# Pairing the 64-wide attention heads on TensorE and splitting the last norm by row blocks

## The reference

```python
h = x                                                   # (1, 256, 1024)
# layer 0
h = h + mixer_mla_retention(rmsnorm(h), ...)            # 8 MLA heads (96 q/k, 64 v), 8 retention heads (64 q/k, 128 v)
h = h + (silu(hn @ w_gate) * (hn @ w_up)) @ w_down      # D_FF = 3584
# layer 1
h = h + mixer_swa_stickbreak(rmsnorm(h), ...)           # 16 window heads and 8 stick-breaking heads, all 64 wide
h = h + moe(rmsnorm(h), ...)                            # top 2 of 8 experts, each SwiGLU with D_FF = 3584
return rmsnorm(h)

# one stick-breaking head, for each block of 128 queries
z = q @ k.T * scale
log_keep = where(before, log_sigmoid(-z), 0)
log_after = cumsum(log_keep, reverse) - log_keep
a = where(before, exp(log_sigmoid(z) + log_after), 0)
out = a @ v
```

## Time and profile before

| | us |
|---|---|
| median of 3 runs | 1602.17 (1601.64 to 1602.81) |
| the profiled execution, device time | 1601.8 |
| its span, first to last instruction | 1599.9 |
| TensorE busy | 1547.9 (97%) |
| TensorE weight loads busy | 1288.1 (81%) |
| VectorE busy | 1235.8 (77%) |
| ScalarE busy | 1085.4 (68%) |
| mean granted TensorE clock | 0.987 of full |

### The profile page before, as it was taken

How to read it: one execution, slowest core, us unless ns; L and a number is a source line. 1 busy time by engine, 2 the same in 40 slices (tenths; PEclk the granted TensorE clock), 3 DMA queues, 4 the chain that set the end, 5 groups by cost and what they waited for, 6 DMA issues and landing times.

```text
span 1599.9 us, 22666 instructions
## 1 busy us (share of the span) xinstructions
PE 1547.9 (97%) x7738; PEld 1288.1 (81%) x7738; DVE 1235.8 (77%) x1456; ACT 1085.4 (68%) x1309; POOL 25.9 (2%) x21
## 2 busy tenths in 40 slices
PE   7999899999999898999999999999999999999995
PEld 6777799999877677888888888888888888888884
DVE  3567544454556547999999999999999999999995
ACT  5555444444455436878878888888878778788874
POOL 0000000000000000000000000000000000000000
PEclk9999999999999998999999999999999999999998
DMA  8533465556443357999999999999999999999950
GB/s 318 184 106 108 138 229 184 184 184 211 159 157 106 118 181 279 365 383 349 399 383 351 393 386 351 395 385 350 394 387 350 392 388 350 394 387 353 404 208 28
DMA packets 193161, 454.90 MB, mean 284 GB/s; under 512 B 8144, under 2 KB 12112, under 8 KB 192848
## 3 DMA queue, kind: packets, MB, share of 16 engines
q1 hardware_dynamic: 190272, 443.69, 75.6%
q0 software_dynamic: 2832, 10.49, 2.6%
HBM read 447.33 MB, written 6.82 MB: 284 GB/s over the span
## 4 chain that ended last, share of the span: by engine, by line
PE 95%; DVE 3%; ACT 1%; issue 1%; DMA 0%; DVEq 0%; ACTq 0%; SPq 0%
PE bank L278 29%; PE bank L280 28%; PE bank L279 28%; PE bank L1757 2%; PE bank L356 1%; DVE w_lo L291 0%; PE bank L1205 0%; PE bank L763 0%; PE bank L752 0%; PE bank L337 0%; PE bank L1197 0%; PE bank L1198 0%; PE bank L357 0%; PE bank L1543 0%; PE bank L1536 0%
## 5 line engine op out<-in xcount | busy, mean ns | idle before, releaser
L291 DVE TENSOR_TENSOR w_lo<-ring,w_hi 128x1024 fp32r<-128x1024 f32 (+1 forms) x834 | 1006.8, 1220 | 255.4 <-ACT w_hi L287 208.9
L287 ACT ACTIVATE w_hi<-ring 128x1024 fp32r<-128x1024 f32 (+1 forms) x834 | 880.7, 1060 | 332.5 <-PE bank L280 332.2
L278 PE MATMUL bank<-w_hi,xe_hi 128*128 128x512 f32 x896 | 354.5, 396 | 3.2 <-DVE w_lo L291 1.8
L280 PE MATMUL bank<-w_hi,xe_lo 128*128 128x512 f32 x896 | 350.3, 391 | 0.0
L279 PE MATMUL bank<-w_lo,xe_hi 128*128 128x512 f32 x896 | 349.5, 390 | 0.0
L278 PEld LDWEIGHTS bank<-w_hi,xe_hi 128*128 128x128 f32 x896 | 168.7, 188 | 37.3 <-DVE w_lo L291 1.9
L280 PEld LDWEIGHTS bank<-w_hi,xe_lo 128*128 128x128 f32 x896 | 168.5, 188 | 36.2
L279 PEld LDWEIGHTS bank<-w_lo,xe_hi 128*128 128x128 f32 x896 | 168.9, 188 | 34.1
L278 PE MATMUL bank<-w_hi,hT_hi 128*128 128x512 f32 x448 | 177.5, 396 | 0.0
L280 PE MATMUL bank<-w_hi,hT_lo 128*128 128x512 f32 x448 | 176.0, 393 | 0.0
L279 PE MATMUL bank<-w_lo,hT_hi 128*128 128x512 f32 x448 | 175.7, 392 | 0.0
(11 more groups left out here) (297 smaller groups left out, 1474.9 us busy)
## 6 DMA issues: line engine op xcount, KB each, us to landing
ring<-m_gate_dram SPq DMA_DIRECT2D x112, 1024.0 KB, 6.0
ring<-m_up_dram SPq DMA_DIRECT2D x112, 1024.0 KB, 6.5
ring<-m_down_dram SPq DMA_DIRECT2D x112, 1024.0 KB, 6.4
ring<-f_gate_dram SPq DMA_DIRECT2D x14, 1024.0 KB, 5.0
ring<-f_up_dram SPq DMA_DIRECT2D x14, 1024.0 KB, 5.0
ring<-f_down_dram SPq DMA_DIRECT2D x14, 1024.0 KB, 4.9
ring<-ab_w_in_dram SPq DMA_DIRECT2D x12, 1024.0 KB, 5.6
ring<-cd_w_in_dram SPq DMA_DIRECT2D x11, 1024.0 KB, 5.0
```

The costliest lines, as they stand in the source:

```text
L278: nc.tensor.matmul(out_, a_hi, b_hi, start=first, stop=False, **kw)
L280: return nc.tensor.matmul(out_, a_lo, b_hi, start=False, stop=last, **kw)
L287: nc.scalar.activation(w_hi[:, buf, 0:width], src, ACT.Copy).then_inc(hi_ready, 1)
L291: nc.vector.tensor_tensor(w_lo[:, buf, 0:width], src, f32(w_hi[:, buf, 0:width]), ALU.subtract).then_inc(split_ready, 1)
```

## The change

1. `heads_out` becomes `pair_out`: it issues the value matmuls of two heads in turn, the first of the even head, the first of the odd head, then the second of each, into the two halves of one bank. MLA's, the window heads' and the stick-breaking heads' value pieces are called once for two heads.
2. The window heads' `scores` and the stick-breaking heads' `z_scores` are issued for two heads in turn, with one signal behind both. A second scores bank is added; the turned probabilities go to bank 6 (the last head's to bank 5) and the window heads' values to bank 7.
3. The pieces move to fit: window scores at odd steps for heads `d` - 7 and `d` - 6, values at even steps for `d` - 10 and `d` - 9; `z_scores` at steps 20, 22, 24, 26; `ln_part`, `softplus` and `log_after` for two heads at steps 21, 23, 25, 27; `masked` and `weights` at the even steps behind; `weigh` at 23, 25, 27, 29. In `ln_part` the three functions go through both heads in turn.
4. The count is waited for and loaded ahead of the last expert (`fullest`). The last norm waits block by block for `h`, squares into its own tile, takes two roots of one column, has its function table loaded ahead, and the result leaves in two DMAs.

The core of the diff:

```diff
+        def pair_out(bank, v, a):
+            for first in (True, False):
+                cols, src = (slice(0, 256), slice(0, 256)) if first else (slice(P, 256), slice(256, 384))
+                for r in range(2):
+                    ins = nc.tensor.matmul(pb[bank][half_rows(r), cols], v[r][0 if first else 1], a[r][:, src],
+                                           start=first, stop=not first, skip_group_check=True)
+            return ins
...
             def ln_part(j):
...
+                for i in (j, j + 1):
+                    act.wait_ge(z_banked, j + 2)
+                    if i >= 3:
+                        act.wait_ge(acc_banked, i - 2)
+                    as_(nc.scalar.activation(sb_sp[i % 3], pb[Z_BANKS[i % 2]][:, 0:384], ACT.Abs))
                 as_.settle()
-                as_(nc.scalar.activation(b, b, ACT.Exp, scale=-1.0))
+                for i in (j, j + 1):
+                    as_(nc.scalar.activation(sb_sp[i % 3], sb_sp[i % 3], ACT.Exp, scale=-1.0))
                 as_.settle()
-                nc.scalar.activation(b, b, ACT.Ln, bias=1.0).then_inc(ln_done, 1)
+                for i in (j, j + 1):
+                    nc.scalar.activation(sb_sp[i % 3], sb_sp[i % 3], ACT.Ln, bias=1.0).then_inc(ln_done, 1)
...
             def weigh(j):
-                pe.wait_ge(a_done, j + 1)
-                if j % 2 == 0 and j:
+                pe.wait_ge(a_done, j + 2)
+                if j:
                     pe.wait_ge(mixT_done, KM + 8 + j // 2)
+                else:
+                    pe.wait_ge(pT_done, MLA_H + SWA_H - 1)
...
+            for tb in range(TB):
+                act.wait_ge(sc_done, 4 + 2 * tb + 2)
+                nc.scalar.activation(squares, h[:, tb, :], ACT.Square, accum_out=ss[:, tb:tb + 1]).then_inc(sq_done, 1)
+                act.wait_ge(sq_done, 8 + tb + 1)
+                nc.scalar.activation(rms[:, tb:tb + 1], ss[:, tb:tb + 1], ACT.Sqrt, bias=const("eps", 0, 1),
+                                     scale=1.0 / D).then_inc(rms_done, 1)
```

More of the change, by code:

```diff
@@ L803, in values @@
             def values(i):
-                pe.wait_ge(pT_done, i + 1)
-                if i % 2 == 0 and i:
+                pe.wait_ge(pT_done, i + 2)
+                if i:
                     pe.wait_ge(mixT_done, i // 2)
-                v0, v1 = (vh[:, tb, i * 64:i * 64 + 64] for tb in range(TB))
-                heads_out(MLA_V, i, v0, v1, pT_sb[i % 2]).then_inc(pv_done, 1)
+                v = [[vh[:, tb, j * 64:j * 64 + 64] for tb in range(TB)] for j in (i, i + 1)]
+                pair_out(MLA_V, v, pT_sb).then_inc(pv_done, 2)
             def ret_scores(i):
@@ L870, in l0_pe @@
                     scores(mla_at(d, 0))
-                if mla_at(d, 2) is not None:
-                    values(mla_at(d, 2))
+                if mla_at(d, 3) is not None and mla_at(d, 3) % 2 == 0:
+                    values(mla_at(d, 3))
                 if mla_at(d, 1) is not None:
@@ L1014, in l1_act @@
             for d in range(L1_UNITS):
-                if 0 <= d - 21 < SB_H:
+                if 0 <= d - 21 < SB_H and d % 2:
                     ln_part(d - 21)
@@ L1034, in l1_act @@
                     exponentials(swa_at(d, 1))
-                if 0 <= d - 22 < SB_H:
+                if 0 <= d - 22 < SB_H and d % 2 == 0:
                     weights(d - 22)
+                    weights(d - 21)
                 if d in (10, 14, 18):
@@ L1101, in l1_dve @@
             for d in range(L1_UNITS):
-                if 0 <= d - 22 < SB_H:
+                if 0 <= d - 22 < SB_H and d % 2 == 0:
                     masked(d - 22)
+                    masked(d - 21)
                 if swa_at(d, 1) is not None:
@@ L1194, in scores @@
                     pe.wait_ge(nm_done, MLA_H + i)
[L1195 to L1198 removed]
+                for out_, tq, tk in ((slice(0, P), slice(0, P), slice(0, P)),
+                                     (slice(P, 384), slice(P, 256), slice(0, 256))):
+                    for j in (i, i + 1):
+                        ins = nc.tensor.matmul(pb[S_BANKS[j % 2]][:, out_], cT[half_rows(j), j // 2, tq],
+                                               cT[half_rows(j), 8 + j // 8, tk], start=True, stop=True)
+                ins.then_inc(s_banked, 2)
             def turn(i):
@@ L1237, in weigh @@
             def weigh(j):
-                pe.wait_ge(a_done, j + 1)
-                if j % 2 == 0 and j:
+                pe.wait_ge(a_done, j + 2)
+                if j:
                     pe.wait_ge(mixT_done, KM + 8 + j // 2)
-                v0, v1 = (bv1[:, tb, j * HD:j * HD + HD] for tb in range(TB))
-                heads_out(SB_BANK, j, v0, v1, sb_a[j % 3]).then_inc(sb_pv, 1)
+                else:
+                    pe.wait_ge(pT_done, MLA_H + SWA_H - 1)
+                v = [[bv1[:, tb, i * HD:i * HD + HD] for tb in range(TB)] for i in (j, j + 1)]
+                pair_out(SB_BANK, v, (sb_a[j % 3], sb_a[(j + 1) % 3])).then_inc(sb_pv, 2)
             for d in range(L1_UNITS):
```

142 lines of the change are left out of this document (70 added, 72 removed).

## The result

The changed kernel took 1582.74 us (median of 4 runs, 1581.6 to 1583.51) beside 1602.49 us for the kernel before (4 runs, 1601.64 to 1602.92): a ratio of 0.9876, 95% interval 0.9861 to 0.9892, 19.75 us less. The forecast was 1582. A second set of the same kernel (the last experiment) gave 1581.44 beside 1602.34. The total was right to within 1 us, partly by luck: its terms were not all right, and in the profiled execution their errors nearly cancelled.

What follows compares the result with a forecast made beforehand. TensorE, busy throughout the window heads and experts, was taken as the bound. Savings of 3.2 + 9.8 + 2.1 + 5.2 = 20.3 us from the profiled 1601.8 gave 1581.5, stated as 1582; range 1575.5 to 1592.

Steps and rivals of the forecast that it cites:

- A pair costs what one head costs: TensorE's paired 64-wide pieces: two heads' scores take 0.86 us and two heads' values 0.81 us.
- Window heads, 9.8: Window-head steps up to step 20: shared scores and values pieces save 10.7 us, less 0.9; bounds 8 and 10.7.
- 0.9 us deducted for late evacuations: Window heads: taken off for VectorE's cT evacuations in steps 13 and 17, 0.35 us each, and a 0.2 us `z_scores` wait.
- MLA, 3.2: MLA's steps: eight values pieces become four, saving 4 x 0.80 us, with nothing giving it back.
- Stick-breaking steps, 2.1: First `z_scores` to last product: 72.9 us becomes 70.8 with two slow-clock charges, 2.1 us saved.
- the walk: Stick-breaking steps laid out anew with measured durations: 65.4 us at full clock, 7.5 less than before.
- the 8.25 us: Steps 21 and 23: the turn comes 8.25 us after the scores, against 6.14 before at step 21.
- the vanished stop of 3.32 us: Step 22: TensorE's old stop at 537.68 goes, since the evacuation behind `turned_copy` now ends at about 10.5.
- I charge 2.7 us for each: Stick-breaking steps: half-clock loss behind each of the first two new stops, 5.4 us in all, none for the third.
- Last norm, 5.2: Tail: second DMA issued 4.5 us earlier and 0.7 us shorter, 5.2 us saved; bounds 3.9 and 7.
- serial column halves: Rival: values pairs run in series, each 0.64 us dearer, 8.3 us over 13 pairs, 1590.2 us; chance 0.18.
- one bank: Rival: two heads in one bank make a values pair cost up to 3.1 us, 1612 in total; chance 0.04.

Runs made afterwards that it cites:

- the last experiment: The changed kernel once more with no edit: 1581.44 us, ratio 0.9863 to the kernel before; its profile is the second profile.
- the clock held up: Changed kernel plus eleven unread matmuls of constants on TensorE ahead of the late turns at steps 21 and 23: 1577.32 us.
- experiments on MLA: Changed kernel with MLA's values pieces again issued one head at a time: 1583.32 us.
- second pass: Changed kernel without the expert overflow pass and its branch, on all engines: 1577.42 us.
- record order: Changed kernel with a pair's records issued head after head instead of in turns: 1582.89 us.
- moved rotations: Changed kernel with VectorE's retention-key rotations at step 16 and behind step 17's normalised probabilities: 1579.6 us.
- split logarithms: Changed kernel, second head's logarithms at steps 21 and 23 behind the exponentials and its softplus behind normalised probabilities: 1574.15 us; together with moved rotations 1573.79 us.
- both heads in the lower half: Changed kernel with both heads' values of a pair written to the lower half of the bank: 1585.61 us.
- the old norm: Changed kernel with the end as before: count loaded behind the addition, one wait, one two-column root, one DMA: 1583.94 us.

## Why the prediction came out right

- **A pair costs what one head costs** (0.86 and 0.81): right. For the column halves it was a choice with no row behind it, against a rule, and so a guess that came true. The Trainium skill ("TensorE: Matmul & The Clock Gate", section "Part 3: Packing small matmuls") says weight loads overlap running matmuls only where the row group differs. Here they share all rows, and 0.81 us for two against 1.44 in one half shows that this rule does not price such a pair. The row there for three column tiles of 32, almost as fast as row tiles, does.
- **Window heads, 9.8**: 10.3. The cause was right and tested by undoing it. The 0.9 us deducted for late evacuations was too much; 10.7 less 10.3 leaves 0.4.
- **MLA, 3.2**: the step that failed is "Its steps are longer than the chain below, so nothing gives it back." At step 18 it was not: VectorE's rotations set the turn, and 0.80 us became a longer stop; 0.70 more went at 115.92. 3.2 - 0.8 - 0.7 = 1.7, and the second profile, without a low stretch, shows 101.32 - 99.37 = 1.95. In the profiled execution a low stretch of 3.4 us behind the longer stop took most of that too. That was the exception: in the second profile and in the seven of experiments that kept MLA's stops, pairs in opposite halves and rotations, the stage took 99.4 us. So the MLA term is 1.9, and the table's 0.3 is one execution's bad luck. The kernel before's trace had the stop of 0.91 us to be seen.
- **Stick-breaking steps, 2.1**: the walk was right, 65.4 at full clock against 65.26 with the clock held up; the order of events, the 8.25 us (8.09) and the vanished stop of 3.32 us in front of the first `output` unit as well. The stops were forecast at 3.7, 3.8 and 2 us and measured 3.32, 3.31 and 1.48. What was mis-sized is "I charge 2.7 us for each". The profiled execution lost 68.34 - 65.26 = 3.1 us for two stretches, half as long as the old one. But the second profile lost 5.4, the 2 x 2.7 predicted, and in it the term is 72.97 - 70.63 = 2.3. In the seven profiles with these steps as changed (the first, the second, and the experiments on MLA, rotations, tail, second pass and record order) the stage took 68.2 or 68.3 us in two and 70.3 to 70.6 in five: the price has two values, and which comes is not set by the code of the stage. So 4.6 in the first profile was a cheap draw, and 2.3 the dearer and more frequent one.
- **The routing was predicted to stay and took 1.5 us more.** No edit touches it. It begins with stops of its own and ran at half clock for 13.65 us instead of 10.24; it took 19.5 to 20.1 us in five of the fourteen profiles, the kernel before's among them, and 21.1 in the other nine, both of the changed kernel among them. This term was missing from the sum; what sets it stays open.
- **Last norm, 5.2**: 6.1 in one pair of profiles, 5.5 to 5.9 by undoing it. The two DMAs took 2.6 us each where 3.2 was assumed, which is most of the surplus.
- **The sum**: MLA 2.9 short, stick-breaking 2.5 over, routing 1.5 short, window heads and tail 1.4 over, and 1.4 lost ahead of MLA and in the dense network: 20.3 predicted, 18.4 between the profiled spans, 19.75 and 20.9 between the medians of the two sets. In the second profile stick-breaking was nearly as forecast and MLA 1.3 short. That the first total came within 1 us is thus luck in part: MLA, the routing and the parts without a term were short by 5.8 us together, and the other terms over by 3.9. The rivals of serial column halves and of one bank are excluded by 0.81 us a pair.

## What to carry to other kernels

Two 64-wide f32 pieces of up to 256 columns in opposite halves of the array cost the time of one, in rows or columns and in either order; but before counting that gain, look for the stops that the shrunk step already has, since step 18, which had one, gave all of it back. Pair on the engine that gains from pairs and leave the operations that feed it one by one: the same pairing brought 0 to 2 us with paired logarithms and 9 to 10 with split ones. Where the clock falls behind a stop, charge the stop twice, once for its length and once for the slow stretch, and give the second a range from several profiles.

## What the runs showed of the hardware beyond this

- The same code with the same stop of 3.3 us went with 3.4 us at half clock in one execution and with 6.8 in another, where the low level began inside the stop. Beginning inside it does not decide the length: with moved rotations it began 0.3 us ahead of the turn and lasted 3.4 us. Stops of 1.4 us at the same place were followed by none in the two versions with split logarithms. A stop of 1.71 us at step 18 was followed by a low stretch in one of nine profiles. A single profile tells such a price only to within 2 us a stage.
- A low stretch ahead of a stop can be free. With both heads in the lower half one ran from 81.7 to 85.1 us, over the unit ahead of step 18's turn, and the turn came 6.09 us behind the last one, as at full clock: the stop took it up.
- The first low stretch of the program ended anywhere from 16.7 to 20.2 us, and the time from the first product to the stop at step 17 was 64.7 us in the profile with both heads in the lower half and 66.3 in the second profile of the changed kernel.
- The branch over the unused second pass held VectorE for 2.78 to 3.05 us in each of the thirteen profiles that have it, and two packets of instructions moved in that gap in the traces of the kernel before, the changed one and the old norm.
